# Two pairs of transformer blocks on one core: where the norm factor of the ups is applied, and the order in which gate weights are summed and split

## The chip, the cores and the metric

The kernel runs on one core of a Trainium2 chip. The metric is the device time of one execution in microseconds (us). TensorE multiplies, VectorE (DVE) and ScalarE (ACT) work on whole tiles, GpSimd (POOL) does elementwise work beside them, and SyncE (SP) issues the DMAs that bring the weights in from HBM.

## The reference, cut to what matters

Input x is 512 tokens by 1024 features in float32. Two layers of a first kind of block run, then two layers of a second kind, then a final RMS norm. The change lies in the feed-forward parts (FFN) of both kinds; the second block has two of them per layer, so there are six FFNs: "ffn" twice, then "ffn1" and "ffn2" twice.

```
# first block, after attention and layer norm 1
f = (jax.nn.silu(x @ w_gate[l]) * (x @ w_up[l])) @ w_down[l]
x = _layernorm(ALPHA * x + f, ln2_g[l], ln2_b[l])
...
# second block: x and half of an FFN of the RMS-normed x, twice (ffn1, then after the mixer ffn2)
def swiglu(x, w_gate, w_up, w_down):
    return (jax.nn.silu(x @ w_gate) * (x @ w_up)) @ w_down
```

w_gate and w_up are 1024 x 2816, w_down is 2816 x 1024. The RMS norm of a token is one factor per token, 1 / sqrt(mean(x*x) + eps), and a gain per feature. Since the factor is the same for all features of a token, it can be multiplied after a matrix product instead of ahead of it.

## The kernel before, in words

Everything is held transposed: 128 features on the partitions, 512 tokens along the free axis. A float32 product is made of three TensorE products of "fp32r" parts: each operand is split into a high part and the rest (hi and lo), and hi*hi, hi*lo and lo*hi are added up in a PSUM bank (mm3, L591 to L593).

**Weights.** They come in units of 128 x 1024 (512 KB) into four slots of `raw`, in a fixed order. SyncE issues unit n when the semaphore w_split says that unit n-4 is split (L533). GpSimd splits most of them in halves: a wait for the slot (with a one-column tensor_tensor, L561), a cast into w_hi (L562), a subtraction into w_lo (L565). GpSimd keeps the order of the units.

**One FFN.** 22 chunks of 128 hidden features. Chunks 0 to 3 (gate0, up0, gate1, up1, each with k = 0, 1) are plain projections of 24 matmuls with 512 columns. Chunks 4 to 21 go in nine pairs. The two gate projections of a pair are made by Strassen's scheme with seven products instead of eight: the weights are the 2 x 2 blocks w11, w12 (slot a) and w21, w22 (slot b), the tokens are two halves of columns, and gate_products (L879) issues the products in the order p1, p6, p7, p5, p2, p4, p3, each 12 matmuls with 256 columns (L867 to L869), into the banks bank_11, bank_22, bank_21 and bank_12. After these the two up projections of the pair follow, plain, into bank_v. Then comes the next pair. After nine pairs, `down` multiplies 8 output chunks of 66 matmuls with 512 columns each.

The gate phases of one FFN begin 20.98 us apart. I call the seven products of a pair its gate phase, and the nine gate phases of an FFN the first, the seven middle and the last one. The six first gate phases begin at 317.48, 935.20, 1300.00, 1867.60, 2221.07 and 2785.59 us.

**What the products wait for.** The weights of the next pair are not split by GpSimd. VectorE makes the sums S1 = w21 + w22 (L2159, into the place of w_lo), S3 = w11 - w21 (L2161), S2 = S1 - w11 (L2163) and S4 = w12 - S2 (L2175); ScalarE rounds them and the raw blocks into hi parts (L1465 to L1478); VectorE subtracts to get the lo parts (pair_a_lo L2169, pair_lo L2189), in the order of LO_PARTS. Each lo part counts in the semaphore weights_lo; when the fourth of five is there (RAW_FREE), GpSimd passes a wait (L554) and lets SyncE load the next gate units into the two slots. The first pair's weights are made ahead of the loop, in first_pair.

The results are combined on VectorE: u2 = p1 + p6 (L2205), u3 = u2 + p7 (L2208), c22 = u3 + p5 (L2212), c21 = u2 + p4 part (L2217), c12 = u2 + p3 part (L2221). u3 and c22 must leave their banks before TensorE may add into them: p4 waits for u3, p3 waits for c22. p2 waits for ScalarE's copy of p1 (keep_p1, L1487). Each engine does its instructions strictly in the order of the code. The sums of the next pair stand behind c22 on VectorE: at once behind it in "ffn"; in ffn1 and ffn2 (ffn_scaled), where the factor scale_by is multiplied in, behind two factor products more (L2334, L2325).

**The factor.** In ffn_scaled a gate gets the factor ahead of the Silu, and each up is multiplied by the factor out of its bank (times_factor, L2001) and then by the gate (L2304), both on VectorE. The down output is added to `resid` by one scalar_tensor_tensor per chunk (L2381, at the end of the kernel L2389), then ScalarE makes xn_hi (L1383) and VectorE xn_lo (L1993) for the next projection.

## Time and profile before

| | us |
|---|---|
| median of 3 runs (3108.43 to 3110.61) | 3109.06 |
| the profiled execution | 3107.27 |
| its span, first to last instruction | 3105.5 |
| PE busy | 3076.8 (99%) |
| POOL busy | 1837.9 (59%) |
| DVE busy | 1738.1 (56%) |
| ACT busy | 923.1 (30%) |

The granted TensorE clock has a mean of 0.998 of full speed.

### The profile page before, as it was taken

What the parts mean: (1) busy time and instruction counts of PE and PEld (TensorE: products, weight loads), DVE (VectorE), ACT (ScalarE), POOL (GpSimd) and SP (SyncE); (2) the same over time, 40 slices, a digit from 0 to 9 for tenths busy, and PEclk for the clock granted to TensorE, in tenths of its full rate; (3) what the DMA queues carried; (4) which work ended last, traced back from release to release, by engine and by line L of the source; (5) the groups of instructions that cost most, each with busy time, mean ns of one, the idle gap of its engine ahead of it and who ended that gap; (6) DMA issues with size and microseconds to landing.
All of it is one profiled execution on the core that took longest, in us unless ns stands there. A gap on an engine that the chain in (4) does not pass through costs nothing.

```text
span 3105.5 us, 46781 instructions
## 1 busy us (share of the span) xinstructions
PE 3076.8 (99%) x17462; PEld 2646.5 (85%) x17462; DVE 1738.1 (56%) x2750; ACT 923.1 (30%) x1800; POOL 1837.9 (59%) x2485
## 2 busy tenths in 40 slices
PE   8999999999999999999999999999999999999999
PEld 7878998898789988899887789988899887789987
DVE  5576545275765452866527567661667336567641
ACT  4454222054542220622212332220323022332210
POOL 5346447673364476544978374478545977374494
PEclk9999999999999999999999999999999999999999
DMA  5112322231123322232332123223222332122231
GB/s 187 48 42 82 108 102 95 95 107 44 42 82 108 106 98 89 75 108 101 102 112 89 48 82 108 102 95 102 95 98 98 103 111 89 41 96 104 92 110 67
DMA packets 83062, 284.53 MB, mean 92 GB/s; under 512 B 9531, under 2 KB 15068, under 8 KB 82652
## 3 DMA queue, kind: packets, MB, share of 16 engines
q1 hardware_dynamic: 77484, 273.70, 26.0%
q10 hardware_dynamic: 5424, 8.79, 0.8%
q8 instruction: 95, 1.56, 0.2%
q14 instruction: 59, 0.48, 0.0%
HBM read 278.79 MB, written 3.67 MB: 91 GB/s over the span
## 4 chain that ended last, share of the span: by engine, by line
PE 94%; DVE 3%; ACT 2%; issue 0%; DMA 0%; DVEq 0%; ACTq 0%
PE bank_v L591 21%; PE bank_v L593 20%; PE bank_v L592 20%; PE bank_s L867 6%; PE bank_s L869 6%; PE bank_s L868 6%; PE bank_a L591 2%; PE bank_a L593 2%; PE bank_a L592 2%; PE bank_v L993 1%; PE bank_a L972 1%; PE bank_s L1133 1%; PE bank_s L1011 1%; PE bank_v L1148 1%; DVE t_sum L2146 0%; PE bank_s L1136 0%
## 5 line engine op out<-in xcount | busy, mean ns | idle before, releaser
L565 POOL TENSOR_TENSOR w_lo<-raw,w_hi 128x512 fp32r<-128x512 f32 x808 | 1085.6, 1344 | 64.6
L591 PE MATMUL bank_v<-xn_hi,w_hi 128*128 128x512 f32 (+1 forms) x1680 | 641.3, 382 | 8.0 <-DVE xn_lo L1934 8.0
L592 PE MATMUL bank_v<-xn_lo,w_hi 128*128 128x512 f32 (+1 forms) x1680 | 635.1, 378 | 0.0
L593 PE MATMUL bank_v<-xn_hi,w_lo 128*128 128x512 f32 (+1 forms) x1680 | 634.8, 378 | 0.0
L561 POOL TENSOR_TENSOR zero<-zero 128x1 f32<-128x1 f32 x808 | 250.0, 309 | 569.0 <-PE bank_v L593 421.0
L562 POOL CAST w_hi<-raw 128x512 fp32r<-128x512 f32 x808 | 545.2, 675 | 0.1
L591 PE MATMUL bank_v<-h_hi,w_hi 128*128 128x512 f32 (+1 forms) x1122 | 422.9, 377 | 0.0
L593 PE MATMUL bank_v<-h_hi,w_lo 128*128 128x512 f32 (+1 forms) x1122 | 422.5, 377 | 0.0
L592 PE MATMUL bank_v<-h_lo,w_hi 128*128 128x512 f32 (+1 forms) x1122 | 422.5, 377 | 0.0
L554 POOL TENSOR_TENSOR zero<-zero 128x1 f32<-128x1 f32 x54 | 28.5, 529 | 602.4 <-DVE w_lo L2189 602.4
L591 PEld LDWEIGHTS bank_v<-xn_hi,w_hi 128*128 128x128 f32 x1680 | 316.7, 189 | 66.1 <-issue 8.7
L593 PEld LDWEIGHTS bank_v<-xn_hi,w_lo 128*128 128x128 f32 x1680 | 316.5, 188 | 59.6
L592 PEld LDWEIGHTS bank_v<-xn_lo,w_hi 128*128 128x128 f32 x1680 | 317.0, 189 | 54.1 <-issue 0.5
L593 PEld LDWEIGHTS bank_v<-h_hi,w_lo 128*128 128x128 f32 x1122 | 211.1, 188 | 38.8
L591 PEld LDWEIGHTS bank_v<-h_hi,w_hi 128*128 128x128 f32 x1122 | 211.1, 188 | 38.7
L592 PEld LDWEIGHTS bank_v<-h_lo,w_hi 128*128 128x128 f32 x1122 | 211.1, 188 | 38.6
L2381 DVE SCALAR_TENSOR_TENSOR resid<-bank_v,resid 128x512 f32<-128x512 f32 x24 | 16.6, 692 | 240.6 <-PE bank_v L593 240.6
L1383 ACT ACTIVATE xn_hi<-resid,par 128x512 fp32r<-128x512 f32 x40 | 28.9, 723 | 364.9 <-DVE resid L2381 323.5
L591 PE MATMUL bank_a<-xn_hi,w_hi 128*128 128x512 f32 (+1 forms) x368 | 133.4, 362 | 3.9 <-ACT work L1516 1.9
L1465 ACT ACTIVATE w_hi<-raw 128x1024 fp32r<-128x1024 f32 x54 | 57.3, 1060 | 268.8 <-PE bank_s L869 259.1
L1487 ACT ACTIVATE parts<-bank_s 128x256 f32<-128x256 f32 x54 | 20.7, 383 | 385.4 <-PE bank_s L869 385.3
L2230 DVE TENSOR_TENSOR h_lo<-hidden,h_hi 128x512 fp32r<-128x512 f32 x132 | 134.3, 1075 | 1.5 <-ACT h_hi L1490 1.5
(413 smaller groups left out, 6419.4 us busy)
## 6 DMA issues: line engine op xcount, KB each, us to landing
raw<-in_w_stream SPq DMA_DIRECT2D x516, 512.0 KB, 3.3
rope<-in_rope ACTq DMA_DIRECT2D x2, 1024.0 KB, 6.2
da_v<-t_rows ACTq DMA_DIRECT2D x2, 1024.0 KB, 7.1
out<-resid SPq DMA_DIRECT2D x8, 256.0 KB, 2.3
t_rows<-t_row ACTq DMA_DIRECT2D x1, 1536.0 KB, 7.2
resid<-in_x ACTq DMA_DIRECT2D x5, 256.0 KB, 7.1
mla_v<-in_alibi ACTq DMA_DIRECT2D x2, 512.0 KB, 6.6
resid<-in_x SPq DMA_DIRECT2D x3, 256.0 KB, 9.3
```

The source lines that it names most:

```text
L561: pool.tensor_tensor(zero[:, 1:2], zero[:, 0:1], zero[:, 0:1], ALU.add)
L562: pool.tensor_copy(w_hi[:, u, cut], raw[:, u, cut]).then_inc(hi_split.sem, 1)
L565: ins = pool.tensor_tensor(w_lo[:, u, cut], raw[:, u, cut], w_hi[:, u, cut].bitcast(F32), ALU.subtract)
L591: pe.matmul(out, lhs_hi, rhs_hi, start=first, stop=False)
L592: pe.matmul(out, lhs_hi, rhs_lo, start=False, stop=False)
L593: return pe.matmul(out, lhs_lo, rhs_hi, start=False, stop=last)
L867: pe.matmul(out, w_h, x_h, start=k == 0 and not more, stop=False, skip_group_check=more)
L868: pe.matmul(out, w_h, x_l, start=False, stop=False, skip_group_check=more)
L869: mm = pe.matmul(out, w_l, x_h, start=False, stop=k == DC // 2 - 1, skip_group_check=more)
L972: mm = pe.transpose(b[:, j * P:(j + 1) * P], source[:, j * P:(j + 1) * P], ident[:, :])
L1465: act.activation(w_hi[:, a, :], raw[:, a, :], ACT.Copy).then_inc(*weights_hi.done((tag, at, "a")))
L2230: dve.tensor_tensor(h_lo[:, f, :], hidden[:, f, :], h_hi[:, f, :].bitcast(F32), ALU.subtract).then_inc(*x_lo.done((tag, "h", f)))
```

## The change: what it does

- ffn_scaled: the ups are no longer multiplied by the factor. An up goes straight from its bank into the product with the gate (one tensor_tensor in place of two; only up0 of the first ffn1 is read from SBUF). The product now holds the bank until the Silu is there. In its place the down output is multiplied by 0.5 and the factor into work[:, 3] and then added to resid: two instructions per chunk (add_half) in place of one.
- The sums of the next pair (S3, S1, S2 and now S4 too) stand on VectorE right behind u3, ahead of c22. They wait for both raw units.
- S1 is written over w21 in `raw` and not into w_lo's place; so S1 and w22 are rounded and split together as "b", one 128 x 1024 operation on each engine. S4 is kept in a PSUM bank (bank_a[0]); for the first pair of an FFN in raw.
- The lo parts are interleaved: S23, then (behind c21) a, then (behind c12) b and S4. GpSimd frees the raw slots after all four parts, where it was the fourth of five.
- ScalarE in ffn_scaled: keep_p1 of the first gate phase stands ahead of the Silu of gate1, k = 1. ScalarE rounds the sums right after keep_p1.
- The first gate phase is taken out of the loops of eight; seven rounds are left. Code for ups in pairs is there but off (UPS_PAIRED is empty).
- A wait for the read of bank_21 stands ahead of p7, and the one for bank_12 is moved to p5.

The core of the diff:

```diff
-LO_PARTS = ("a", "S23", "S1", "A22", "S4")
...
+LO_PARTS = ("S23", "a", "b", "S4")
...
-        w_sum, = overlay(("w_sum", [P, SLOTS, UNIT], F32))
...
+        def last_sum_place(tag, at, side):
+            return raw[:, side_slots(tag, side)[0], KEPT:UNIT] if at == "first" else bank_a[SIDES.index(side)][:, :]
...
-                if n in GATE_UNITS:
-                    pool.wait_ge(weights_lo.sem, len(LO_PARTS) * GATE_UNITS[n] + RAW_FREE)
+                if n in PAIRED_UNITS:
+                    pool.wait_ge(weights_lo.sem, len(LO_PARTS) * (PAIRED_UNITS[n] + 1))
+                    pool.wait_ge(w_split.sem, split_count(n - 1))
...
+                pe.wait_ge(*c21_read.before((*key, "c21")))
...
+            def b_hi(tag, at, side):
+                _, b = side_slots(tag, side)
+                act.wait_ge(*weights_summed.after((tag, at, side, "S1")))
+                act.activation(w_hi[:, b, :], raw[:, b, :], ACT.Copy).then_inc(*weights_hi.done((tag, at, side, "b")))
...
+            def last_sum_hi(tag, at, side):
+                act.wait_ge(*weights_summed.after((tag, at, side, "S4")))
+                act.activation(side_sums(side)[3], last_sum_place(tag, at, side), ACT.Copy).then_inc(*weights_hi.done((tag, at, side, "S4")))
...
+                def gate_side(at, j):
+                    key = (tag, at, "gate")
+                    keep_p1(key)
...
+                    else:
+                        sums_hi(tag, at, "gate")
+                    act.wait_ge(*multiplied.after((*key, "p2")))
+                    act.wait_ge(*combined.after((*key, "c22")))
+                    act.activation(work[:, 0, HALVES[0]], bank_11, ACT.Silu).then_inc(*c11_read.done((*key, "c11")))
...
+                        a_hi(tag, at, "gate", j + 1)
+                        act.wait_ge(*multiplied.after((*key, "p4")))
+                        b_hi(tag, at, "gate")
...
+                        act.wait_ge(*multiplied.after((*key, "p3")))
+                        last_sum_hi(tag, at, "gate")
...
+                def gate_out(n, k):
+                    if n:
+                        act.wait_ge(*(product.after((tag, "h0", k)) if kept else v_read.after((tag, "up0", k))))
+                    if n or not kept:
+                        leave_bank((tag, f"gate{n}", k))
...
+                    if (n, k) != (1, 1):
+                        gate_out(n, k)
...
+                def gate_side(at, j):
+                    key = (tag, at, "gate")
+                    keep_p1(key)
+                    if at == "zero":
+                        gate(1, 1)
...
+            def weight_sums(tag, at, side, j):
+
+                a, b = side_slots(tag, side)
+                _, _, total, _, _ = side_sums(side)
                 w11, w21, w22 = raw[:, a, 0:KEPT], raw[:, b, 0:KEPT], raw[:, b, KEPT:UNIT]
-                dve.wait_ge(raw_in[b].sem, pair_raw(tag, j))
-                dve.tensor_tensor(w_sum[:, b, 0:KEPT], w21, w22, ALU.add).then_inc(*weights_summed.done((tag, at, "S1")))
-                dve.wait_ge(raw_in[a].sem, pair_raw(tag, j))
-                dve.tensor_tensor(s_sum[:, 1, :], w11, w21, ALU.subtract).then_inc(*weights_summed.done((tag, at, "S3")))
-                dve.wait_ge(*weights_summed.after((tag, at, "S1")))
-                dve.tensor_tensor(s_sum[:, 0, :], w_sum[:, b, 0:KEPT], w11, ALU.subtract
-                                  ).then_inc(*weights_summed.done((tag, at, "S2")))
-
-            def pair_a_lo(tag, at):
-                a, _ = pair_slots(tag)
-                dve.wait_ge(*weights_hi.after((tag, at, "a")))
+                key = (tag, at, side)
+                dve.wait_ge(raw_in[a].sem, side_raw(tag, side, j))
+                dve.wait_ge(raw_in[b].sem, side_raw(tag, side, j))
+                dve.tensor_tensor(total[:, 1, :], w11, w21, ALU.subtract).then_inc(*weights_summed.done((*key, "S3")))
+                dve.tensor_tensor(w21, w21, w22, ALU.add).then_inc(*weights_summed.done((*key, "S1")))
+                dve.wait_ge(*weights_summed.after((*key, "S1")))
+                dve.tensor_tensor(total[:, 0, :], w21, w11, ALU.subtract).then_inc(*weights_summed.done((*key, "S2")))
+                if at != "first":
+                    dve.wait_ge(*weights_summed.after((*key, "S2")))
+                    last_sum(tag, at, side)
+
...
-                dve.tensor_tensor(s_sum[:, 2, :], raw[:, a, KEPT:UNIT], s_sum[:, 0, :], ALU.subtract
-                                  ).then_inc(*weights_summed.done((tag, at, "S4")))
...
+                dve.tensor_tensor(last_sum_place(tag, at, side), raw[:, a, KEPT:UNIT], total[:, 0, :], ALU.subtract
+                                  ).then_inc(*weights_summed.done((tag, at, side, "S4")))
...
+                lo, whole, hi = dict(S23=(s23_lo, s23_sum, s23_hi), b=(w_lo[:, b, :], raw[:, b, :], w_hi[:, b, :]),
+                                     S4=(s4_lo, last_sum_place(tag, at, side), s4_hi))[name]
...
-                pair_sums(tag, "first", 0)
-                pair_a_lo(tag, "first")
-                pair_last_sum(tag, "first")
-                for name in LO_PARTS[1:]:
-                    pair_lo(tag, "first", name)
+                weight_sums(tag, "first", "gate", 0)
+                a_lo(tag, "first", "gate")
+                dve.wait_ge(*weights_lo.after((tag, "first", "gate", "a")))
+                last_sum(tag, "first", "gate")
+                for name in ("S23", "b", "S4"):
+                    side_lo(tag, "first", "gate", name)
...
+            def combine_22(key, c22, behind=lambda name: None):
...
+                dve.tensor_tensor(u2, parts[:, 0, :], bank_22, ALU.add).then_inc(*combined.done((*key, "u2")))
...
+                dve.wait_ge(*multiplied.after((*key, "p7")))
+                dve.wait_ge(*combined.after((*key, "u2")))
+                dve.tensor_tensor(u3, u2, bank_21, ALU.add).then_inc(*combined.done((*key, "u3")))
+                behind("u3")
+                dve.wait_ge(*multiplied.after((*key, "p5")))
+                dve.wait_ge(*combined.after((*key, "u3")))
+                dve.tensor_tensor(c22, u3, bank_12, ALU.add).then_inc(*combined.done((*key, "c22")))
+                behind("c22")
...
+                    def behind(name):
+                        if name == "u3" and more:
+                            weight_sums(tag, at, "gate", j + 1)
+                        ahead(name)
+
+                    combine_22(key, work[:, 1, HALVES[1]], behind)
+                    if more:
+                        side_lo(tag, at, "gate", "S23")
+                    ahead("c11")
+                    combine_21(key, work[:, 1, HALVES[0]])
+                    if more:
+                        a_lo(tag, at, "gate")
+                    combine_12(key, work[:, 0, HALVES[1]])
+                    ahead("c12")
+                    if more:
+                        side_lo(tag, at, "gate", "b")
+                        side_lo(tag, at, "gate", "S4")
 
...
                 def first(n, k):
-                    up = (tag, f"up{n}", k)
+                    up, at = (tag, f"up{n}", k), slice(2 * n + k, 2 * n + k + 1)
                     times_factor(work[:, k, :], value.done((tag, f"gate{n}", k)), a_read.after((tag, f"gate{n}", k)))
+                    dve.wait_ge(*gated.after((tag, f"gate{n}", k)))
                     if n or not kept:
-                        times_factor(work[:, 2 + k, :], v_read.done(up), w_used.after(up), v_bank(up)[:, :])
+                        dve.wait_ge(*w_used.after(up))
+                        ins = dve.tensor_tensor(hidden[:, at, :], work[:, k:k + 1, :], v_bank(up)[:, :].unsqueeze(1), ALU.mult)
+                        ins.then_inc(*v_read.done(up))
+                    else:
                         dve.wait_ge(*v_read.after(up))
...
+                        ins = dve.tensor_tensor(hidden[:, at, :], work[:, k:k + 1, :], work[:, 2 + k:3 + k, :], ALU.mult)
+                        ins.then_inc(*product.done((tag, f"h{n}", k)))
...
+                    combine_22(key, work[:, 1, HALVES[1]], behind)
+                    dve.wait_ge(*multiplied.after((*key, "p2")))
...
                     dve.tensor_tensor(work[:, 0, HALVES[0]], bank_11, scale_by[:, HALVES[0]], ALU.mult
...
+                                      ).then_inc(*c11_read.done((*key, "c11")))
+                    if more:
+                        side_lo(tag, at, "gate", "S23")
+                    ahead("c11")
+                    combine_21(key, work[:, 1, HALVES[0]])
+                    dve.wait_ge(*c21_read.after((*key, "c21")))
+                    scale_part(1, slice(0, S), value.done((*key, "c21")))
+                    if more:
+                        a_lo(tag, at, "gate")
+                    combine_12(key, work[:, 0, HALVES[1]])
+                    dve.wait_ge(*c12_read.after((*key, "c12")))
+                    scale_part(0, HALVES[1], value.done((*key, "c12")))
+                    ahead("c12")
+                    if more:
+                        side_lo(tag, at, "gate", "b")
+                        side_lo(tag, at, "gate", "S4")
...
+            def add_half(key, cut, previous=None):
+                if previous:
+                    dve.wait_ge(*v_read.after(previous))
+                step(dve.scalar_tensor_tensor(out=work[:, 3, cut], in0=v_bank(key)[:, cut], scalar=0.5, in1=scale_by[:, cut],
+                                              op0=ALU.mult, op1=ALU.mult), (*key, "scaled"))
+                dve.tensor_tensor(resid[:, key[2], cut], resid[:, key[2], cut], work[:, 3, cut], ALU.add
+                                  ).then_inc(*v_read.done(key))
+
...
-                    key = (tag, "down", c)
                     dve.wait_ge(*down_ready(tag, c))
-                    dve.scalar_tensor_tensor(out=resid[:, c, :], in0=v_bank(key)[:, :], scalar=0.5,
-                                             in1=resid[:, c, :], op0=ALU.mult, op1=ALU.add).then_inc(*v_read.done(key))
+                    add_half((tag, "down", c), slice(0, S), (tag, "down", c - 1) if c else None)
```

## Rows read from the trace of the kernel before

**Rows 1.** Page: busy us by engine (share, instructions); shares of the chain.

```profile
PE 3076.8 (99%) x17462; PEld 2646.5 (85%) x17462; DVE 1738.1 (56%) x2750; ACT 923.1 (30%) x1800; POOL 1837.9 (59%) x2485
PE 94%; DVE 3%; ACT 2%; issue 0%; DMA 0%; DVEq 0%; ACTq 0%
```

**Rows 2.** Waits of PE in 1300 to 1315 us: total us, times, longest.

```profile
PE bank_s L867 <- ACT parts L1487: 1.9, 1, 1.9
PE bank_s L867 <- DVE parts L2208: 0.6, 1, 0.6
```

**Rows 3.** Timeline of PE (start, us, operation): first matmuls of p1 and p3.

```profile
317.48 0.28 PE L867 MATMUL bank_s<-xn_hi,w_hi 128*128 128x256 f32 x1
...
326.12 0.28 PE L867 MATMUL bank_s<-xn_hi,s_hi 128*128 128x256 f32 x1
```

**Rows 4.** Timeline of DVE, a middle gate phase (it begins at 1407.95).

```profile
1412.57 0.42 DVE L2208 TENSOR_TENSOR parts<-parts,bank_s 128x256 f32<-128x256 f32 x1 [1.12 <-PE bank_s L869]
...
1416.02 0.69 DVE L2159 TENSOR_TENSOR w_sum<-raw 128x512 f32<-128x512 f32 x1
1416.62 0.69 DVE L2161 TENSOR_TENSOR s_sum<-raw 128x512 f32<-128x512 f32 x1
```

**Rows 5.** Timelines of DVE and PE, 1309 to 1311: u3 and p4.

```profile
1309.61 0.42 DVE L2208 TENSOR_TENSOR parts<-parts,bank_s 128x256 f32<-128x256 f32 x1
...
1310.16 0.38 PE L867 MATMUL bank_s<-t_hi,w_hi 128*128 128x256 f32 x1 [0.62 <-DVE parts L2208]
```

**Rows 6.** Timeline of POOL, the same middle gate phase.

```profile
1412.41 1.30 POOL L565 TENSOR_TENSOR w_lo<-raw,w_hi 128x512 fp32r<-128x512 f32 x1
1424.94 0.51 POOL L554 TENSOR_TENSOR zero<-zero 128x1 f32<-128x1 f32 x1 [11.23 <-DVE w_lo L2189]
```

**Rows 7.** Timeline of DVE, first gate phase of the first FFN.

```profile
318.19 0.68 DVE L2189 TENSOR_TENSOR s_lo<-s_sum,s_hi 128x512 fp32r<-128x512 f32 x1
...
323.86 1.67 DVE L2159 TENSOR_TENSOR w_sum<-raw 128x512 f32<-128x512 f32 x1
...
326.06 1.09 DVE L2163 TENSOR_TENSOR s_sum<-w_sum,raw 128x512 f32<-128x512 f32 x1
```

**Rows 8.** Timeline of POOL, the same stretch.

```profile
317.28 1.04 POOL L554 TENSOR_TENSOR zero<-zero 128x1 f32<-128x1 f32 x1 [9.57 <-DVE w_lo L2189]
...
323.70 1.29 POOL L565 TENSOR_TENSOR w_lo<-raw,w_hi 128x512 fp32r<-128x512 f32 x1
...
325.53 1.08 POOL L562 CAST w_hi<-raw 128x512 fp32r<-128x512 f32 x1
```

**Rows 9.** Weight DMAs (L533) issued in 317 to 320 us, and their landing.

```profile
L533 SPq DMA_DIRECT2D raw<-in_w_stream x2: 328/380/432, 318.3 to 318.7; - x2
DMA to landing us min/median/max: 3.3/3.8/4.3
```

**Rows 10.** Landing of the two units issued in 935 to 937, 2785 to 2787.

```profile
DMA to landing us min/median/max: 3.6/4.3/5.1
...
DMA to landing us min/median/max: 3.2/4.4/5.7
```

**Rows 11.** Timelines of DVE and POOL, ffn2 of the first layer.

```profile
1846.04 0.69 DVE L2001 TENSOR_TENSOR work<-bank_v,scale_by 128x512 f32<-128x512 f32 x1 [4.12 <-PE bank_v L593]
1846.77 1.67 DVE L2304 TENSOR_TENSOR hidden<-work 128x512 f32<-128x512 f32 x1
...
1867.44 0.51 POOL L554 TENSOR_TENSOR zero<-zero 128x1 f32<-128x1 f32 x1 [15.17 <-DVE w_lo L2189]
```

**Rows 12.** The chain at the end; DVE and PE behind a down.

```profile
3096.76 0.43 DVE resid L2389
...
1613.25 1.22 DVE L1993 SCALAR_TENSOR_TENSOR xn_lo<-resid,par,xn_hi 128x512 fp32r<-128x512 f32 x1 [0.79 <-ACT xn_hi L1383]
...
1616.33 0.39 PE L591 MATMUL bank_a<-xn_hi,w_hi 128*128 128x512 f32 x1
```

**Rows 13.** Windows: stretch, its length, busy of engines (instructions), PEclk, DMA, GB/s.

```profile
1278.00:1282.00 4.00, 4.00 (x13) 3.19 (x13) 3.40 (x5) 1.58 (x4) 3.92 (x6) 0.61 0.33 95
```

More of the change, by code:

```diff
@@ L66 @@
                   ffn2=[DEPTH * B1_UNITS + B2_UNITS * l + FFN_UNITS + B2_PROJ + DC for l in range(DEPTH)])
-GATE_UNITS = {}
-for start in FFN_STARTS["ffn"] + [FFN_STARTS[tag][l] for l in range(DEPTH) for tag in ("ffn1", "ffn2")]:
+UPS_PAIRED = ()
+PAIRED_UNITS = {}
+for tag, start in sorted(((tag, start) for tag in FFN_STARTS for start in FFN_STARTS[tag]), key=lambda entry: entry[1]):
     for j in range(PAIRED):
-        GATE_UNITS[start + 2 * PLAIN + 4 * j] = len(GATE_UNITS)
-LO_PARTS = ("a", "S23", "S1", "A22", "S4")
+        for side in range(2 if tag in UPS_PAIRED and 0 < j < PAIRED - 1 else 1):
+            PAIRED_UNITS[start + 2 * PLAIN + 4 * j + 2 * side] = len(PAIRED_UNITS)
+SIDES = ("gate", "up")
+LO_PARTS = ("S23", "a", "b", "S4")
 H_ORDER = (2, 3, 4, 5, 0, 1, *range(6, FC))
@@ L910, in second_hidden @@
+                side_products(tag, "last", "gate", PAIRED - 1)
+                plain_ups("last")
             def second_hidden(tag):
@@ L1550, in ffn @@
                 gate(1, 1)
-                with loop(act, tag, PAIRED - 1) as i:
-                    pair("pair", i)
-                pair("last", None)
-                hidden_hi_rest(tag, ready)
+                all_pairs(tag, gate_side, gate_half)
             def keep_scaled_x(column, c):
@@ L1599, in ffn_scaled, with gate_half @@
+                    if at != "last":
+                        act.wait_ge(*multiplied.after((*key, "p3")))
+                        last_sum_hi(tag, at, "gate")
+                def gate_half(at):
+                    key = (tag, at, "gate")
+                    act.wait_ge(*value.after((*key, "c12")))
+                    act.activation(work[:, 0, :], work[:, 0, :], ACT.Silu).then_inc(*gated.done((*key, 0)))
                 if kept:
@@ L1609, in ffn_scaled @@
                     first_pair_hi(tag)
-                gate(1, 1)
-                with loop(act, tag, PAIRED - 1) as i:
-                    pair("pair", i)
-                pair("last", None)
-                hidden_hi_rest(tag, ready)
+                gate_out(1, 1)
+                all_pairs(tag, gate_side, gate_half)
             def write_sink(key, n, k):
@@ L2364, in ffn_scaled @@
                 first(1, 1)
-                with loop(dve, tag, PAIRED - 1) as i:
-                    pair("pair", i)
-                    for k in range(2):
-                        finish("pair", k, bass.ds(i * 2 + (PLAIN + k), 1))
-                pair("last", None)
-                rest(lambda k: finish("last", k, slice(FC - 2 + k, FC - 1 + k)))
+                all_pairs(tag, gate_side)
             def down_ready(tag, c):
```

451 lines of the change are left out of this document (244 added, 207 removed).

## The prediction

> **What bounds the kernel.** I read the page first. TensorE is busy in 3076.8 of 3105.5 us and carries 94% of the chain that ended last; VectorE and GpSimd, whose work is edited here, are at 56% and 59% [rows 1]. So VectorE work that goes or comes is worth nothing by itself: only a wait of TensorE counts. Next I read the waits of TensorE by place. Of 54 gate phases, 53 have none: p1 to p7 follow at 1.44 us, p3 starts 8.64 us after p1 (317.48 to 326.12) [rows 3]. Only the first gate phase of the first ffn1 (at 1300.0) waits, 1.9 us for keep_p1 and 0.6 for u3 [rows 2]; its p3 starts 11.69 after p1, 3.05 late. That is all the change can win. Then I followed, in the timelines of VectorE and GpSimd, how much room each wait of TensorE in a gate phase has.
>
> **The ups without the factor: nothing.** Per up one VectorE instruction goes (0.69) and one with two SBUF inputs becomes one with a PSUM input. None of these stands in front of TensorE in the middle phases. The up bank is now held until the Silu is done; the next user of it comes a gate phase (10.1 us) later, so nothing waits.
>
> **The down output in two instructions: +0.5.** Behind a down, the last xn_lo ends at 1613.25 + 1.22 = 1614.47, and TensorE needs it at 1616.33 [rows 12]: 1.86 us of room. The added instruction costs 0.69, with a GpSimd operation of up to 1.3 in its way at the worst 2.0; I take 0. At the end of the kernel nothing covers it: a half chunk takes 0.43 [rows 12], a second one the same and a hand-over of 0.04. +0.46.
>
> **Sums ahead of c22, middle phases: nothing.** u3 starts 1412.57 - 1407.95 = 4.62 into the phase and ends at 5.04 [rows 4]. Behind it now stand S3, S1, S2 and S4: instructions of 0.69 follow each other at 0.60 [rows 4], two of them wait for the result ahead (+0.08 each), so c22 starts at 4.96 + 2.6 = 7.6 and ends at 8.02. From the end of u3 to p4's first matmul it took 1310.16 - 1310.03 = 0.13 [rows 5]. p3 could start at 8.15 and is due at 8.64: 0.5 us of room where there were 2. The raw units must be there at 4.96 and GpSimd must be quiet. In ffn1 and ffn2 GpSimd's last subtraction now ends at 1413.71, 5.76 into the phase, since its four splits start only at L554, 16.99 into a phase: 9.75 us from there to the end [rows 6]. In the new order the last lo part of a middle phase is done by 13 us in ffn and 15 us in ffn1 and ffn2; L554 moves there, the splits end by 2 to 4 us into the next phase, and the weights land over 5 us early. So 0 for 42 middle phases. The last phases have no sums; in them nothing changes for TensorE.
>
> **Sums ahead of c22, first phases: this is the cost.** Here two covers are gone.
>
> (a) The raw units come late. The first pair's lo parts free the slots only shortly before the phase. At 317.48, L554 starts at 317.28, ends at 318.32, and the two units are issued at 318.3 and 318.7; the second lands 4.3 later, at 323.0, 5.5 into the phase [rows 8, 9]. Before, the sums started at 323.86 and did not see it; now they want it at 4.96. And L554 has to wait for the fifth part, S4's lo, too: it ended at 318.87 [rows 7] and with two dependent waits more in first_pair I put it at 318.98, L554 from 319.12 to 319.63. That is 1.3 later than before, so the second unit lands 6.8 into the phase. At 935.2 the same two units took up to 5.1 [rows 10]: 7.6. In the ffn2 phases the chain ahead of first_pair gets shorter: a pair of instructions of 0.69 and 1.67 at 1846.04 [rows 11] becomes one of 0.69, all behind it is 1.7 earlier, and L554, at 1867.44 before [rows 11], comes near 1866.55: the second unit lands at 4.0, in time. At 2785.6 it took 5.7 [rows 10] and lands at 5.5. At 2221.1 the gain is 0.7; it lands at 3.2.
>
> (b) GpSimd is at work. Behind L554 it splits four halves, in first phases until 8 to 12 us into the phase. Where both have an operation on SBUF, one waits until the other's is over: S1, begun at 323.86, lasted until 325.53, 0.54 behind the end of GpSimd's subtraction of 323.70; then a cast took 1.08, and the sum beside it 1.09 instead of 0.69 [rows 4, 7, 8]. Four sums with waits between them let GpSimd in three or four times: the rest of an operation, a cast (0.5) and a subtraction (1.2). Sum 1.8 to 2.9, I take 2.3; if GpSimd happens to be idle, 0. For S4 written to PSUM no row shows such a wait; with two SBUF inputs I count it like the others (without it, 1.2 less per phase at most).
>
> The Trainium skill bears on S4 (SBUF — State Buffer, "SBUF: two separate sides"): an operation with two SBUF inputs takes the shared pair exclusively against a GpSimd one that reads SBUF, wherever it writes. By it S4 is held up as well; only without it would a phase be up to 1.2 us cheaper. That DVE instructions with a PSUM input are not held up, the trace shows: u3 lasts 0.42 beside GpSimd's work too.
>
> So c22 ends at (time of S3) + 2.6 + 2.3 + 0.42, and p3 starts 0.13 later instead of at 8.64. Loss per first phase, as low / taken / high:
> - 317.5: S3 at 6.9: 1.5 / 3.0 / 4.4 (there I followed the two queues one by one: c22 ends at 11.5)
> - 935.2: S3 at 7.6: 2.2 / 3.4 / 5.1
> - 1867.6: S3 at 4.96: 0 / 1.7 / 2.4; 2221.1: 0 / 1.6 / 2.4
> - 2785.6: S3 at 5.5: 0.1 / 2.0 / 3.0
> - 1300.0: keep_p1 now stands ahead of the Silu, so the 1.9 goes. But the product of up 1 waits for that Silu, u3 ends near 8.5, p4 waits 1.5, and the sums behind u3 push c22 to near 12.8: p3 is 4.3 late instead of 3.05. -0.8 / +1.2 / +2.4.
>
> Sum: 13.0 (3.0 to 19.7), with the tail 13.4 (3.5 to 20.2). On the profiled execution that gives 3107.27 + 13.4 = 3120.7; the median of the runs is 1.8 above it, so 3109.06 + 13.4 = 3122.5.
>
> **Rivals.**
>
> 1. Little happens (3110 to 3115, taken 3112.6). The sums meet GpSimd between its operations and the units land sooner, since less DVE work lies ahead of first_pair: the low ends above. For it: VectorE is rid of an instruction per up. Against: GpSimd runs four halves back to back behind L554 in all six first phases.
>
> 2. Not slower, by one mechanism: keep_p1. In the phase at 1300.0 the 3.05 us go fully, and c22 arrives by 8.5 in the other five. 3109.06 - 3.05 + 0.46 = 3106.5. It decides at 0.5 us: all four sums must be through 3.1 us behind u3 (they need 2.6 with nobody in the way). Against it: landings at 5.5 and later [rows 9, 10], which alone break it in two phases.
>
> 3. The middle phases pay as well. If GpSimd's last subtraction stays at 5.76 in ffn1 and ffn2 [rows 6], S3 begins 0.75 later, c22 ends at 8.77 and p3 starts at 8.90: 0.27 x 28 phases = 7.6 on top, 3130.1. For it: 0.5 us of room is little, and any slip repeats 28 or 42 times. Against it: the last lo part moves up by 2 to 4 us.
>
> 4. The clock. In 1278 to 1282 the granted clock was 0.61 of full speed [rows 13], so most of that stretch ran at the lower level, 1.2 GHz, behind waits of TensorE for the norm's sums. A stall of 3 us ahead of p3 might bring such a stretch of some 3 us, about 1.6 us each; one or two are inside my range.
>
> **Numbers.** My forecast has 0.72, rival 1 0.14, rival 2 0.04, rival 3 0.10. A measurement of this kernel tells 0.2% (6.2 us) from no change: slower means above 3115.3, faster below 3102.8. Rival 1 is mostly inside that band, rival 2 wholly; my own low ends add a little. Slower 0.83, same 0.14, faster 0.03. The range 3112 to 3130 goes from the low bounds (3112.6) to the high ones (3129.3) with a clock stretch.
>
> **What would show it.** In the changed profile: TensorE's waits, nearly absent before, are headed by waits for c22 (the sum u3 + p5 on VectorE) ahead of p3, six times, 1 to 4 us each, and none in middle phases. The ffn phases at 317 and 935 pay most, and there S3 starts at a landing. The sums last 1.1 to 1.8 instead of 0.69. L554 of middle phases starts near 13 (ffn) and 15 (ffn1, ffn2) us into the phase. The last step before the output is 0.46 longer. I am wrong if p3 starts 8.64 after p1 in the first phases, or if middle phases take longer than 20.98 us.

## The result, and the profile after

The changed kernel takes 3127.96 us (median of 4, 3127.44 to 3128.33); the kernel before, on the same chip between them, 3108.74 (median of 4, 3107.87 to 3110.61). The ratio is 1.0063, 95% interval [1.0051, 1.0076]: 19.2 us slower. The forecast was 3122.5, range 3112 to 3130, slower 0.83. The profiled execution took 3127.86 with a span of 3126.0, against 3107.27 and 3105.5 before; the traces thus have 20.5 us to account for. Medians here and below are of the fast runs; one run of e2 (6988 us) and one of e3 (4486 us), far above the rest, are left out.

The page of after, its busy times and chain, answers to [rows 1]. VectorE and GpSimd do less and TensorE's share of the chain still falls from 94% to 92%, because VectorE, ScalarE and waits come into it.

```profile
PE 3081.6 (99%) x17462; PEld 2650.7 (85%) x17462; DVE 1638.3 (52%) x2605; ACT 909.9 (29%) x1746; POOL 1801.1 (58%) x2485
PE 92%; DVE 4%; ACT 2%; issue 1%; DMA 1%; DVEq 0%; SPq 0%; ACTq 0%; POOL 0%; POOLq 0%
```

The waits of TensorE in the whole of after (total us, times, longest). The first line is new: six waits for c22, which is the sum at L2310, before p3. The second is the wait for u3 at the start of the first ffn1 phase [rows 2]; the wait for keep_p1 there (1.9) is down to 0.3. The third lies at the end of the kernel.

```profile
PE bank_s L885 <- DVE work L2310: 15.7, 6, 4.2
...
PE bank_s L885 <- DVE parts L2306: 1.8, 1, 1.8
PE bank_s L823 <- ACT work L1392: 1.4, 1, 1.4
```

Now the first gate phase of the first FFN. TensorE's timeline answers to [rows 3]: p1 at 318.42, p3 at 331.37, 12.95 later instead of 8.64, and a wait of 4.16 in front of it.

```profile
318.42 0.28 PE L885 MATMUL bank_s<-xn_hi,w_hi 128*128 128x256 f32 x1
...
331.37 0.55 PE L885 MATMUL bank_s<-xn_hi,s_hi 128*128 128x256 f32 x1 [4.16 <-DVE work L2310]
```

VectorE's timeline of the same phase is where the four sums stand (S3, S1, S2, S4 at L2252, L2253, L2255, L2271) between u3 and c22. VectorE is idle for 3.27 us behind u3, until a weight transfer has landed; then the first two sums take 1.15 and 1.75 instead of 0.69.

```profile
322.93 0.42 DVE L2306 TENSOR_TENSOR parts<-parts,bank_s 128x256 f32<-128x256 f32 x1 [0.92 <-PE bank_s L887]
326.62 1.15 DVE L2252 TENSOR_TENSOR s_sum<-raw 128x512 f32<-128x512 f32 x1 [3.27 <-DMA raw<-in_w_stream]
327.69 1.75 DVE L2253 TENSOR_TENSOR raw<-raw 128x512 f32<-128x512 f32 x1
329.47 0.69 DVE L2255 TENSOR_TENSOR s_sum<-raw 128x512 f32<-128x512 f32 x1
330.20 0.70 DVE L2271 TENSOR_TENSOR bank_a<-raw,s_sum 128x512 f32<-128x512 f32 x1
330.81 0.41 DVE L2310 TENSOR_TENSOR work<-parts,bank_s 128x256 f32<-128x256 f32 x1
```

GpSimd's timeline shows both causes [rows 8]: the release of the slots (L570) comes at 320.12 instead of 317.28, and behind it a cast and a subtraction lie on the two long sums.

```profile
320.12 0.19 POOL L570 TENSOR_TENSOR zero<-zero 128x1 f32<-128x1 f32 x1 [11.48 <-DVE s_lo L2284]
...
326.61 0.61 POOL L578 CAST w_hi<-raw 128x512 fp32r<-128x512 f32 x1
327.30 1.58 POOL L581 TENSOR_TENSOR w_lo<-raw,w_hi 128x512 fp32r<-128x512 f32 x1
```

The line of SyncE's transfers in 318 to 322 us answers to [rows 9]: issued at 320.3 and 320.7, and the second took 5.8 us where it had taken 4.3.

```profile
L548 SPq DMA_DIRECT2D raw<-in_w_stream x2: 328/380/431, 320.3 to 320.7; - x2
...
DMA to landing us min/median/max: 3.2/4.5/5.8
```

A middle gate phase, whose p1 starts at 1423.72, answers to [rows 4]. With nobody in the way S3 to c22 takes 1431.34 - 1428.68 = 2.66; c22 ends 8.03 into the phase and p3 starts on time, at 8.63. GpSimd is silent here from 1426.1 to 1438.08. All 42 middle phases begin 20.98 us before the next one, as in the kernel before.

```profile
1428.34 0.42 DVE L2306 TENSOR_TENSOR parts<-parts,bank_s 128x256 f32<-128x256 f32 x1 [1.12 <-PE bank_s L887]
1428.68 0.69 DVE L2252 TENSOR_TENSOR s_sum<-raw 128x512 f32<-128x512 f32 x1
...
1431.34 0.41 DVE L2310 TENSOR_TENSOR work<-parts,bank_s 128x256 f32<-128x256 f32 x1
...
1438.08 0.19 POOL L570 TENSOR_TENSOR zero<-zero 128x1 f32<-128x1 f32 x1 [12.00 <-DVE s_lo L2284]
```

The windows of after (stretch, length, busy of PE, PEld, DVE, ACT, POOL, granted clock, DMA) answer to [rows 13]. Time at 1.2 instead of 2.4 GHz is (1 - clock) x 2 x length: 3.4 us at 277, 6.8 at 328, 3.4 each at 953 and 1325, together 17.0; the last three lie in or right behind a wait for c22, the first has TensorE busy all the time. The long one begins at 329.2, 2.1 us ahead of the end of the wait for c22, so 4.7 us of it fall on work. The stretch of before at 1278 is gone (1.00).

```profile
277.00:282.00 5.00, 5.00 (x31) 5.00 (x31) 3.47 (x13) 2.04 (x5) 0.00 (x0) 0.66 0.01 3
328.00:337.00 9.00, 5.63 (x21) 5.09 (x22) 8.00 (x10) 4.75 (x7) 1.08 (x2) 0.62 0.17 59
953.00:958.00 5.00, 4.54 (x19) 4.15 (x20) 4.95 (x7) 3.58 (x6) 0.00 (x0) 0.66 0.32 105
1278.00:1282.00 4.00, 4.00 (x36) 4.00 (x35) 2.76 (x6) 2.76 (x9) 1.51 (x3) 1.00 0.00 0
1325.00:1330.00 5.00, 4.14 (x17) 3.89 (x18) 4.93 (x9) 2.81 (x4) 0.00 (x0) 0.66 0.33 108
```

By the same sum over its windows, before has three such stretches of 3.4 us: at 36, at 828 and the one of [rows 13].

```profile
36.00:40.00 4.00, 4.00 (x11) 3.17 (x12) 3.87 (x5) 3.47 (x5) 3.57 (x4) 0.57 0.91 311
828.00:832.00 4.00, 4.00 (x35) 3.27 (x35) 2.27 (x6) 1.24 (x6) 0.00 (x0) 0.57 0.00 0
```

The account, from the starts of p1 and p3 on TensorE: p3 of the six first phases is later by 16.8 us in all (table below). Time at the lower clock is 6.8 us longer; 2.1 of it passed in the wait at 329, so it costs (6.8 - 2.1) / 2 = 2.3 us of work. The stretch behind the last first phase is 0.4 longer, with one instruction more in the tail (0.46). And the first p1 of the first FFN starts 0.9 later (318.42 against 317.48). That last term is not the change's: in the twelve traces this p1 starts between 316.9 and 318.6, and in after TensorE is 1.5 us behind already at 36 us, in the attention. Together 20.4, against 20.5 measured.

### The profile page after: what moved, and what is told of

It reads as the page before. It is cut to its first block, busy times and chain, and to the rows that moved or that the text cites. A ratio compares the mean times of both kernels' runs of the same rounds, so it can differ in the third digit from the quotient of the medians.

```text
span 3126.0 us, 46287 instructions
## 1 busy us (share of the span) xinstructions
PE 3081.6 (99%) x17462; PEld 2650.7 (85%) x17462; DVE 1638.3 (52%) x2605; ACT 909.9 (29%) x1746; POOL 1801.1 (58%) x2485
## 3 DMA queue, kind: packets, MB, share of 16 engines
q8 instruction: 102, 1.67, 0.2%
## 4 chain that ended last, share of the span: by engine, by line
PE 92%; DVE 4%; ACT 2%; issue 1%; DMA 1%; DVEq 0%; SPq 0%; ACTq 0%; POOL 0%; POOLq 0%
PE bank_v L607 20%; PE bank_v L608 20%; PE bank_v L609 20%; PE bank_s L885 5%; PE bank_s L887 5%; PE bank_s L886 5%; PE bank_a L607 2%; PE bank_a L609 2%; PE bank_a L608 2%; PE bank_v L1033 1%; PE bank_a L1012 1%; PE bank_s L1173 1%; PE bank_s L1051 1%; PE bank_v L1188 1%; PE bank_s L1176 0%
## 5 line engine op out<-in xcount | busy, mean ns | idle before, releaser
L577 POOL TENSOR_TENSOR zero<-zero 128x1 f32<-128x1 f32 x808 | 233.0, 288 | 617.5 <-PE bank_v L609 456.9
L578 POOL CAST w_hi<-raw 128x512 fp32r<-128x512 f32 x808 | 532.5, 659 | 0.2
L570 POOL TENSOR_TENSOR zero<-zero 128x1 f32<-128x1 f32 x54 | 11.7, 217 | 610.9 <-DVE s_lo L2284 460.7
L2355 DVE TENSOR_TENSOR hidden<-work,bank_v 128x512 f32 (+1 forms) x116 | 79.6, 687 | 356.7 <-PE bank_v L609 350.4
L2525 DVE SCALAR_TENSOR_TENSOR work<-bank_v,scale_by 128x512 f32<-128x512 f32 (+1 forms) x33 | 22.3, 675 | 316.2 <-PE bank_v L609 316.2
L1505 ACT ACTIVATE s_hi<-s_sum 128x1024 fp32r<-128x1024 f32 x54 | 57.3, 1062 | 263.9 <-DVE s_sum L2255 263.9
```

Of the source, the lines that this page charges most:

```text
L577: pool.tensor_tensor(zero[:, 1:2], zero[:, 0:1], zero[:, 0:1], ALU.add)
L578: pool.tensor_copy(w_hi[:, u, cut], raw[:, u, cut]).then_inc(hi_split.sem, 1)
L1505: act.activation(hi, total, ACT.Copy).then_inc(*weights_hi.done((tag, at, side, "S23")))
L2355: dve.tensor_tensor(hidden[:, at, :], work[:, k:k + 1, :], v_bank(up)[:, :].unsqueeze(1), ALU.mult).then_inc(*v_read.done(up))
```

## The experiments

"p3 late" is the first matmul of p3 less that of p1 less 8.63, from TensorE's timeline, for the six first phases in order; "half clock" is the time at 1.2 GHz, the kernel's last microseconds left out. The last column takes p3's lateness and half of the half-clock time off the span, leaving out what of that time TensorE waited (2.1 us in after, 0.8 in e9 and in e11): it stays between 3097.2 and 3100.0, so these two terms carry all but 2.8 us of what the kernels differ by. Most of the rest is the opening: counted from the first FFN's first p1, with only the half-clock time behind it, the remainder is 2781.5 to 2782.3 in all twelve. Each ratio is to runs of before taken with that kernel (medians 3107.9 to 3108.7).

| kernel | median us | ratio to before | p3 late, us | sum | half clock | span less both |
|---|---|---|---|---|---|---|
| before | 3108.1 | | 0, 0, 3.1, 0, 0, 0 | 3.1 | 10.2 | 3097.3 |
| after | 3127.96 | 1.0063 | 4.3, 3.7, 7.6, 1.7, 0.9, 1.7 | 19.9 | 17.0 | 3098.6 |
| e1 first behind c22 | 3107.56 | 0.9998 | 0, 0, 1.7, 0, 0, 0 (and 0.6) | 2.3 | 10.2 | 3098.6 |
| e2 all behind c22 | 3106.26 | 0.9994 | 0, 0, 1.7, 0, 0, 0 | 1.7 | 10.2 | 3098.6 |
| e3 GpSimd quiet | 3112.86 | 1.0018 | 3.1, 1.7, 4.7, 0, 0, 0 | 9.4 | 3.4 | 3099.1 |
| e4 slots early | 3121.84 | 1.0044 | 1.9, 3.1, 7.3, 1.4, 0.7, 1.4 | 15.9 | 10.2 | 3099.0 |
| e5 both | 3109.44 | 1.0004 | 0.2, 0.7, 3.0, 0, 0, 0 | 3.9 | 13.6 | 3098.8 |
| e6 fourth behind | 3116.01 | 1.0026 | 2.1, 2.1, 6.0, 0, 0, 0 | 10.2 | 10.2 | 3097.2 |
| e7 ups alone | 3105.55 | 0.9993 | 0, 0, 1.6, 0, 0, 0 | 1.6 | 6.8 | 3098.7 |
| e9 stall filled | 3126.37 | 1.0060 | 4.3, 3.7, 7.6, 1.7, 0.9, 1.7 | 20.0 | 13.6 | 3098.6 |
| e10 best | 3104.79 | 0.9990 | 0, 0, 0.6, 0, 0, 0 | 0.6 | 6.8 | 3100.0 |
| e11 fourth in SBUF | 3127.43 | 1.0062 | 3.8, 3.7, 7.7, 1.7, 0.9, 1.7 | 19.5 | 13.6 | 3098.6 |

### Undoing one line: the sums behind c22 (e1, e2)

```diff
-                        if name == "u3" and more:
+                        if name == ("c22" if at == "zero" else "u3") and more:   # e1
+                        if name == "c22" and more:                               # e2
                             weight_sums(tag, at, "gate", j + 1)
```

> The kernel after, but in the first gate phase of each FFN the four sums for the next pair stand behind the third combination (c22) on VectorE; in the middle phases they stay ahead of it. Theory A (what the prediction says: VectorE reaches c22 late because of sums that wait for late units and run beside GpSimd): the waits of p3 for c22 go in all six first phases, 4.3 + 3.7 + 4.4 + 1.7 + 1.0 + 1.7 = 16.8 us of stall, and the stretches at half clock behind them go too (about 3 us): 3107.5 to 3110 us, at 1300 only the lateness up to p4 stays (2 to 3 us). Rival B (the loss is in the ups, in the down step's two instructions or in the order of the low parts): 3126 us or more, as after. Rival C (the stall only moves to what was behind the sums, the low parts for the second pair): 3115 to 3125 us, with new waits of p1 or p6 in the first middle phase.

> As the first of these runs, and in the 48 middle gate phases too the sums stand behind c22. Theory A (in the middle phases the sums fit in the room ahead of p3): within 1 us of the run with only the first phases changed, 3107.5 to 3111 us. Rival B (the middle phases pay as well, 0.1 us or more each, hidden in the matmul rows): 4 us or more below that run.

Measured: e1 3107.56 (ratio to before 0.9998 [0.9988, 1.0007]), e2 3106.26 (0.9994 [0.9984, 1.0004]). Theory A held: with only the place of the sums in six phases undone, nothing that can be measured is left of the loss. VectorE's timeline of e1 in the first phase shows it plainly. The sums still wait for the same late landing and are still long (S4 1.68), but c22 is through at 324.5, 1.5 us ahead of the first of them.

```profile
322.63 0.42 DVE L2306 TENSOR_TENSOR parts<-parts,bank_s 128x256 f32<-128x256 f32 x1 [0.92 <-PE bank_s L887]
324.07 0.42 DVE L2310 TENSOR_TENSOR work<-parts,bank_s 128x256 f32<-128x256 f32 x1 [1.02 <-PE bank_s L887]
325.99 0.80 DVE L2252 TENSOR_TENSOR s_sum<-raw 128x512 f32<-128x512 f32 x1 [1.50 <-DMA raw<-in_w_stream]
...
328.45 1.68 DVE L2271 TENSOR_TENSOR bank_a<-raw,s_sum 128x512 f32<-128x512 f32 x1
```

Between e1 and e2 lie 1.3 us by the medians and 0.6 by the spans; that is a little more than the 1 us expected, and far less than rival B's 4. The 0.6 is one phase, the second of the first ffn1 (p3 0.6 late in e1); the other 41 middle phases, and the six last ones, are on time in both. So rival 3 of the prediction is out.

### The two causes apart (e3, e4, e5)

e3 and e5 leave out the split of two up units of each FFN but for one column; what they show is timing alone. e5 has the edits of e3 and e4 together.

```diff
-pool.tensor_copy(w_hi[:, u, cut], raw[:, u, cut])...        # e3, for the two up units behind each FFN's first gate pair:
+pool.tensor_copy(w_hi[:, u, one column], ...)                #   the subtraction likewise

-return raw[:, side_slots(tag, side)[0], KEPT:UNIT] if at == "first" else ...        # e4
+return s_sum[:, 2, :] if at == "first" else ...
-pool.wait_ge(weights_lo.sem, len(LO_PARTS) * (PAIRED_UNITS[n] + 1))
+pool.wait_ge(weights_lo.sem, len(LO_PARTS) * (PAIRED_UNITS[n] + 1) - (n in FIRST_UNITS))
...
-dve.wait_ge(*weights_lo.after((tag, "first", "gate", "a")))
+dve.wait_ge(*weights_summed.after((tag, "first", "gate", "S2")))
```

> The kernel after, but GpSimd's copy and subtraction of the two up units that it splits during each first gate phase do one column of 1024 only; so the split of two of an FFN's units is left out. Order of VectorE unchanged. Theory A (contention with GpSimd makes the sums 1.0 to 1.8 us long instead of 0.6 to 0.7, landing does the rest): the four sums take 0.55 to 0.75 us each, 2.0 to 2.4 us less per phase; the waits at 1867, 2221 and 2785 go, those at 317 and 935 fall to 1.5 to 2.5 us, that at 1300 by 1.5 to 3 us: 3114 to 3119 us. Rival B (only the late landing counts, the long sums are an effect of their operands or of PSUM): within 2 us of after, sums as long as before.

> The kernel after, but the fourth sum of the first pair goes to a tile of its own, so the raw slots of the first gate pair are handed back after the third of its four low parts and the next units are fetched about 0.7 us earlier. Theory A (landing decides the start of the sums at 317, 935 and 1300): their first sum starts 0.6 to 0.9 us earlier in these three and p3's wait falls by as much; at 1867, 2221 and 2785, where u3 at 4.9 starts the sums, nothing changes: 1.5 to 4 us below after, 3124 to 3126.5 us. Rival B (VectorE starts the sums by its own queue everywhere): within 0.6 us of after. Rival C (an earlier fetch makes GpSimd's next units land together with them, later than before): the same or slower.

> The kernel after with both earlier edits: GpSimd does one column of the two units that it splits in each first gate phase (the split of two of an FFN's units is left out), and the raw slots are handed back after the third low part. Theory A (landing and contention together are the whole lateness of c22 at 317 and 935; the earlier fetch alone had drawn GpSimd's work over the sums): the sums start at 5.5 to 6 us and take 0.7 each, c22 ends at 8.6 to 9 us, p3 waits 0 to 0.5 us at 317 and 935, 0 behind, and 3 to 4.5 us at 1300: 3108 to 3111 us. Rival B (some of the lateness has another cause, such as the semaphores between the sums): 1 us or more of p3's wait left at 317 and 935.

Measured: e3 3112.86 (1.0018 [1.0008, 1.0028]), 1.1 below theory A's range, with only one stretch at half clock. The three phases that had no landing to wait for (1867, 2221, 2785) are on time, and at 317 only the landing is left. VectorE's timeline of e3 there: the first sum again begins at a landing, but all four take 0.68 to 0.70, and S3 to c22 is 2.66 us, as in a middle phase. GpSimd is thus the whole of the sums' lengthening.

```profile
326.97 0.69 DVE L2260 TENSOR_TENSOR s_sum<-raw 128x512 f32<-128x512 f32 x1 [3.53 <-DMA raw<-in_w_stream]
327.58 0.68 DVE L2261 TENSOR_TENSOR raw<-raw 128x512 f32<-128x512 f32 x1
...
329.02 0.70 DVE L2279 TENSOR_TENSOR bank_a<-raw,s_sum 128x512 f32<-128x512 f32 x1
329.63 0.41 DVE L2318 TENSOR_TENSOR work<-parts,bank_s 128x256 f32<-128x256 f32 x1
```

e4 took 3121.84 (1.0044 [1.0028, 1.0061]), 6.1 below after, where 1.5 to 4 were expected: the sums began 2.7 us earlier at 317 and 1.0 at 935, not 0.6 to 0.9. The release itself moved from 1.7 to -0.2 us, since it no longer waits for S4's low part, which stands behind an instruction of 1.2 us. But in VectorE's timeline the second cause takes part of it back: beginning at 323.90, S2 and S4 now meet GpSimd (1.67 and 1.12), and S3 to c22 takes 4.5 us.

```profile
323.90 0.69 DVE L2253 TENSOR_TENSOR s_sum<-raw 128x512 f32<-128x512 f32 x1 [0.59 <-DMA raw<-in_w_stream]
324.51 1.10 DVE L2254 TENSOR_TENSOR raw<-raw 128x512 f32<-128x512 f32 x1
325.65 1.67 DVE L2256 TENSOR_TENSOR s_sum<-raw 128x512 f32<-128x512 f32 x1
327.35 1.12 DVE L2272 TENSOR_TENSOR bank_a<-raw,s_sum 128x512 f32<-128x512 f32 x1
328.38 0.41 DVE L2311 TENSOR_TENSOR work<-parts,bank_s 128x256 f32<-128x256 f32 x1
```

e5 took 3109.44 (1.0004 [0.9995, 1.0014]), as theory A said: 0.2 and 0.7 us are left at 317 and 935 (up to 0.5 expected), none behind, 3.0 at 1300. Landing and GpSimd together are, but for these 0.9 us, the lateness of c22 in five of the six phases.

### Three sums ahead, and where the fourth is kept (e6, e11)

```diff
-                if at != "first":                                              # e6
+                if at not in ("first", "zero"):
...
+                        if name == "c22" and at == "zero":                     # e6: S4 here, S3, S1, S2 stay ahead
+                            last_sum(tag, at, "gate")
...
-            return raw[...] if at == "first" else bank_a[SIDES.index(side)][:, :]        # e11
+            return raw[...] if at == "first" else su_sum[:, 0, :]
```

> The kernel after, but in the first gate phase of each FFN only the fourth sum stands behind c22; the other three stay ahead of it. Theory A (each instruction ahead of c22 delays p3 by its own length as long as p3 waits): p3's lateness falls by S4's length with its gap, 0.7 us at 317, 1.7 at 935 and at 1300, and goes at 1867, 2221 and 2785 (1.7 + 1.0 + 1.7), 8.4 us of stall in all: 3118 to 3121 us. Rival B (the first sum's start, by the landing, is what counts, and the others get through together): 3 us or less below after. Rival C (GpSimd takes the freed time, the other sums get longer): 3121 to 3125 us.

> The kernel after, but from the first phase on the fourth sum is kept in an SBUF tile instead of a bank; order as in after. Theory A (an operation with two SBUF inputs is held up by GpSimd wherever it writes): S4 takes as long as in after, 1.65 us in four of the six first phases and 0.7 in the others; p3's waits change by less than 0.3 us each, its low part, with two SBUF inputs now, may get longer but nothing of TensorE waits for it: within 1.5 us of after. Rival B (the bank is what makes S4 long): S4 at 0.7 us everywhere, up to 1 us less in five phases, 3122 to 3125 us. Rival C (the bank spares something behind the sums): 2 us or more above after.

Measured: e6 3116.01 (1.0026 [1.0016, 1.0036]), 2 us better than theory A's range: the stall fell by 9.7 us instead of 8.4, since at 317 it fell by 2.2 and not 0.7: S1 escaped GpSimd this time (0.68 instead of 1.75). Less time at half clock (10.2 us instead of 17.0) saves 2.4 us more. e11 3127.43 (1.0062 [1.0046, 1.0079]), within 0.6 of after. VectorE's line of S4 in the phase at 1882, kept in SBUF, has the length that it has in the bank in the same phase of after (1.66): the place of the fourth sum is no part of the loss, nor a gain.

```profile
1890.06 1.66 DVE L2271 TENSOR_TENSOR su_sum<-raw,s_sum 128x512 f32<-128x512 f32 x1
```

The Trainium skill (SBUF — State Buffer, "SBUF: two separate sides") ties this to the inputs: a VectorE operation with two SBUF inputs and a GpSimd operation that reads SBUF shut each other out, and it sets no condition on where the result goes. The traces agree, with 1.66 us for either place against 0.70 when GpSimd is quiet.

### The other half of the change alone (e7)

The kernel before, with its order of sums, and only the ups without the factor and the down step in two instructions.

> The kernel before with the other half of the change alone: in the second block the ups are multiplied from their bank without the norm factor, and the down step is two instructions. Order and places of the weight sums as before. Theory A (VectorE's saved factors lie beside TensorE; only the last down half stands on the path): 0.3 to 0.7 us more than before in the tail; at 1300, where VectorE has a backlog at the start, the product now waits for Silu in order, which may cost or spare up to 1 us: -0.5 to +1.2 us in all, p3's wait for c22 nowhere. Rival B (part of the 19 us is here): 3 us or more above before.

Measured: 3105.55, 0.9993 [0.9984, 1.0002]: no loss here, perhaps 2 us of gain, which the interval doesn't tell from none; the median is 2.5 below before, outside theory A's -0.5 to +1.2. Its trace has p3 1.6 late at 1300 instead of 3.1, since u3 ends 8.5 into the phase and not 10.0, and one stretch at half clock less; the tail's 0.46 is in it. Of TensorE's waits in e7 one line is left there, with 1.4 instead of the 1.9 and 0.6 of [rows 2]:

```profile
PE bank_s L867 <- ACT parts L1487: 1.4, 1, 1.4
```

### Do TensorE's waits bring the lower clock? (e9)

```diff
+                if at == "zero" and tag == "ffn":
+                    for _ in range(24):
+                        pe.matmul(spare[:, HALVES[0]], xn_hi[:, 0, 0:P], xn_hi[:, 0, HALVES[0]], start=True, stop=True)
                 split("S4")
                 pe.wait_ge(*combined.after((*key, "c22")))
```

> The kernel after, but in the two first gate phases of the first block (317 and 935) TensorE does 24 extra matmuls of 256 columns, 2.9 us of work whose result is thrown away, ahead of its wait for c22 of 4.3 and 3.7 us; so it idles 1.4 and 0.8 us there. At 1300 and behind nothing changes. Theory A (the stretches at half clock right behind the waits follow from TensorE's idling): the 6.8 us at 329 and the 3.4 us at 954 go, the one behind 1326 stays; p3 is as late as before, and the time falls by 3.4 to 5.1 us, to 3123 to 3124.5 us, unless a stretch comes elsewhere instead. Rival B (the stretches come by themselves, whatever TensorE did ahead of them): as many stretches as in after, time within 1 us of it. Rival C (the extra work delays p3): above after.

Measured: 3126.37 (1.0060 [1.0045, 1.0076]), 1.6 below after; p3 is as late as before. The windows of e9: no lower clock at 329 and 952, where after had 6.8 and 3.4 us of it, but 3.4 us at 899, in plain projections with TensorE busy all the time, and 6.8 instead of 3.4 at 1322.

```profile
329.00:337.00 8.00, 6.69 (x41) 5.83 (x40) 7.11 (x10) 4.65 (x7) 0.71 (x4) 1.00 0.21 67
899.00:904.00 5.00, 5.00 (x32) 5.00 (x31) 3.28 (x12) 2.12 (x5) 0.00 (x0) 0.66 0.00 0
952.00:958.00 6.00, 5.43 (x30) 4.78 (x31) 5.17 (x8) 3.59 (x6) 0.62 (x3) 1.00 0.30 90
1322.00:1330.00 8.00, 6.56 (x23) 5.78 (x24) 7.41 (x11) 4.04 (x6) 0.61 (x2) 0.57 0.20 66
```

Theory A is half right: in this one trace the two filled waits have no such stretch behind them. But 6.8 of the 10.2 us came up elsewhere, and the time is above theory A's 3123 to 3124.5. What decides where and how often the clock falls stays open; from the twelve traces only this can be said: ahead of the kernel's end it is down for 3.4 us at a time, twice for 6.8 (after, e9), 3.4 to 17.0 us a run. Where TensorE has work all through, 3.4 us cost 1.6: so much longer than in before is the way from p3 to the next p1 at 954 and at 1326 in after.

### A version that beats both (e10)

e2, and in the second block's first(1, 1) the product is issued behind u3 of the first gate phase instead of ahead of it.

> A version meant to beat both: the sums behind c22 in every gate phase, and in the second block the product of the last of the first four chunks moved behind u3 of the first gate phase, so that at 1300 u2 and u3 don't stand behind that product's wait for Silu. Theory A: the lateness left at 1300 in the run with all sums behind c22 (p3 1.7 us late, all of it p4 waiting for u3) falls by 0.7 to 1.7 us, no p3 waits anywhere: 0.7 to 1.7 us below that run, 3105 to 3107 us, no difference from before that can be measured or 1 to 2 us faster. Rival B (u3 there waits for the first pair's splits, not for the product): no change against that run. Rival C (c22 now behind product and u3): p3 late again by 0.3 us or more in some first phase.

Measured: 3104.79, 0.9990 [0.9981, 0.9999] against before (3108.07), 0.1% faster, by an interval that only just leaves out none; 1.5 us below e2. In VectorE's timeline at 1300, u3 stands ahead of the product (L2469), which had to wait for the Silu, and p3 is 0.6 late instead of 1.7:

```profile
1307.90 0.42 DVE L2306 TENSOR_TENSOR parts<-parts,bank_s 128x256 f32<-128x256 f32 x1 [0.46 <-DVE parts L2302]
1308.24 0.68 DVE L2469 TENSOR_TENSOR hidden<-work,bank_v 128x512 f32<-128x512 f32 x1
1308.95 0.42 DVE L2310 TENSOR_TENSOR work<-parts,bank_s 128x256 f32<-128x256 f32 x1
```

## Why the prediction was right, and where its sizes were off

- **The mechanism.** Six waits for c22, none in the 42 middle phases, c22 through at 8.03 there (8.02 said), and all of it undone by e1. This was shown. The release in middle phases comes 13.1 us into them in ffn (13 said) and 14.3 in ffn1 and ffn2 (15 said).
- **(a) Landing.** The second unit lands 8.1 into the phase at 317 (6.8 said) and 6.5 at 935 (7.6 said). The release came when it was put (end at 1.9, 2.15 said); what missed is the transfer, 5.8 us and 4.2 instead of 4.3 and 5.1. The two errors nearly cancel in the sum, which is luck. At 1867, 2221 and 2785 the units are there at 4.3, 3.7 and 4.3, ahead of u3's end, as said for two; the 5.5 said for 2785 took over a transfer of 5.7 us, which now took 4.1.
- **(b) GpSimd.** S3 to c22 less the 2.66 of a quiet phase is 1.5, 2.5, 2.8, 2.2, 1.5, 2.3: mean 2.1, against 2.3 taken and bounds of 1.8 to 2.9, the low one too high.
- **Five phases without 1300:** 12.3 us, 11.7 taken. The prediction did not keep to its own formula, (time of S3) + 2.6 + 2.3 + 0.42 + 0.13 - 8.64: at 935 it gives 4.4, where 3.4 was taken, and at 2785 2.3, where 2.0 was taken. The six taken values add up to 12.9, not 13.0.
- **The phase at 1300 is the term that was mis-sized:** +4.6 instead of +1.2, above its high bound of 2.4. About half is (b), 2.8 for the sums where the 12.8 for c22 had left 1.3. That is a slip in the working: with the 2.3 of (b), u3 at 8.5 gives c22 at 13.8, a term of +2.2 and a high bound of 2.9. The rest, 1.8, is u3, and it goes with the clock. The prediction had u3 end near 8.5; in e1, the same program up to there, it ends at 8.7, in after at 10.3. In the runs with a stretch at half clock at 1278 to 1284 (before, e1, e2, e5, e7, e10) the release of the slots comes 2.6 to 3.4 us into the phase, in those without (after, e3, e4, e6, e9, e11) 4.2 to 5.0. I read it so: VectorE has a backlog there that it brings from the norm; when TensorE loses 1.7 us to the lower clock on its way to p1, VectorE has caught up by as much. All twelve traces fit, but no run set the clock on purpose. The prediction took this stretch of before [rows 13] as given.

VectorE's timeline of after at 1300 shows this backlog and then the sums: the factor of the second chunk 1.35 long, its product waiting for the Silu, u3 at last at 1319.50 (the phase began at 1309.60), and all four sums drawn out.

```profile
1316.33 1.35 DVE L2091 TENSOR_TENSOR work<-work,scale_by 128x512 f32<-128x512 f32 x1
1318.37 0.69 DVE L2465 TENSOR_TENSOR hidden<-work,bank_v 128x512 f32<-128x512 f32 x1 [0.70 <-ACT work L1665]
...
1319.50 0.42 DVE L2306 TENSOR_TENSOR parts<-parts,bank_s 128x256 f32<-128x256 f32 x1
1319.83 1.04 DVE L2252 TENSOR_TENSOR s_sum<-raw 128x512 f32<-128x512 f32 x1
1320.79 1.77 DVE L2253 TENSOR_TENSOR raw<-raw 128x512 f32<-128x512 f32 x1
1322.60 1.11 DVE L2255 TENSOR_TENSOR s_sum<-raw 128x512 f32<-128x512 f32 x1
1323.74 1.65 DVE L2271 TENSOR_TENSOR bank_a<-raw,s_sum 128x512 f32<-128x512 f32 x1
```

- **The clock** was a rival with no term in the sum, one or two stretches of 1.6 us in the range. It was 6.8 us more at half clock, and 2.3 us of work, since part of it fell into a wait.
- **The tail:** +0.46. The chain at the end of after has two instructions where [rows 12] had one of 0.43; the wait behind them grew from 1.0 to 1.4. From the last first phase to the end it is 0.4 in all.

```profile
3116.84 0.43 DVE work L2525
...
3117.30 0.44 DVE resid L2527
```

- **The ups: nothing** by the sum; e7 bears that out within its interval, but for the phase at 1300, where u3 ends at 8.5 with them alone, as the prediction had it. The wait for keep_p1 at 1300 went nearly whole (0.3 left), as said, and brought nothing, since u3 and the sums were later than it.

Between the 13.4 predicted and the 20.5 of the traces lie 7.1 us: 3.4 are the phase at 1300, 2.3 the clock, 0.6 the other five phases and 0.9 the opening, which is not the change's; the tail is 0.1 less. The medians differ by 1.3 less than the two profiled executions.

## What to carry to other kernels

Moving filler work ahead of an instruction that the busiest engine waits for needs a cover for each kind of pass of the loop, and the first pass is the one to work out: its operands were ordered late, and the neighbour engine is still catching up. Here 42 passes had room, and 6 cost 0.6%. Where two engines slow each other down, bringing the work forward may only move it into the other's busy time (e4); putting the short instruction that is awaited ahead of the long filler cost nothing here (e1, e10). And where a forecast has a formula, put every case through it: at 1300 the term taken left out nearly half of the sums' lengthening.
